# Products nobody reads, in the waits of TensorE, in a two-layer decoder trunk

## The reference, cut to what matters

```
x = x + gla_mixer(rmsnorm(x, c_norm[i]), c_w_in[i], c_w_a2[i], c_b_a[i], c_o_norm[i], c_w_out[i])
x = x + moe_ffn(rmsnorm(x, m_norm[i]), m_router[i], m_w_gate[i], m_w_up[i], m_w_down[i])
...
log_a = (jax.nn.log_sigmoid((a1 @ w_a2 + b_a).astype(jnp.float32)) / GLA_TAU).reshape(B, S, H, dk)
...
att = jnp.einsum('bhid,bhjd,bhijd->bhij', qc, kc, decay)
...
logits = (xt @ router).astype(jnp.float32)
top_v, top_i = lax.top_k(logits, TOP_K)
top_w = jax.nn.softmax(top_v, axis=-1)
```

## Time and profile before

| | |
|---|---|
| three executions | 1360.69, 1359.76, 1362.06 us |
| span of the profiled execution | 1358.3 us |
| TensorE products busy | 1297.8 us (96%) |
| weight loads busy | 1063.5 us (78%) |
| DVE, ACT, POOL busy | 1046.4, 814.9, 31.9 us |
| mean granted clock of TensorE | 0.973 |
| chain that ended last | PE 90%, DVE 5%, ACT 2%, issue 1%, POOL 1% |

### The profile page before, as it was taken

One profiled execution on the slowest core, in us unless ns is written; L12 is line 12 of the kernel. 1 busy time (PEld: TensorE's weight loads), 2 busy tenths in 40 slices (PEclk: granted clock), 3 DMA queues, 4 the chain that ended last, 5 costly groups with the idle time before them and its releaser, 6 DMA issues.

```text
span 1358.3 us, 17178 instructions
## 1 busy us (share of the span) xinstructions
PE 1297.8 (96%) x6105; PEld 1063.5 (78%) x6111; DVE 1046.4 (77%) x1014; ACT 814.9 (60%) x847; POOL 31.9 (2%) x29
## 2 busy tenths in 40 slices
PE   6999999999989997899999999999999999999997
PEld 5877878888778766688888888788887888888885
DVE  4786664444477945788998989889989889989986
ACT  5434354444335434577767767777776777777773
POOL 0130000000011000000000000000000000000000
PEclk9989999999989978799999999999999999999999
DMA  9540045554524302399999999999999899989992
GB/s 386 216 152 5 1 158 187 187 187 186 189 100 166 129 32 93 140 364 346 368 349 339 366 355 341 342 344 347 358 341 361 332 338 362 350 344 365 343 373 89
DMA packets 48635, 350.75 MB, mean 258 GB/s; under 512 B 5392, under 2 KB 5392, under 8 KB 6320
## 3 DMA queue, kind: packets, MB, share of 16 engines
q1 hardware_dynamic: 48560, 349.67, 68.5%
HBM read 348.60 MB, written 1.05 MB: 257 GB/s over the span
## 4 chain that ended last, share of the span: by engine, by line
PE 90%; DVE 5%; ACT 2%; issue 1%; POOL 1%; DMA 0%; SPq 0%; POOLq 0%; DVEq 0%; ACTq 0%
PE bank L490 26%; PE bank L492 26%; PE bank L491 26%; PE bank L922 1%; PE bank L652 1%; PE bank L798 1%; PE bank L678 1%; DVE wlo L1280 1%; ACT whi L1012 1%; PE bank L660 1%; PE bank L873 1%; PE bank L874 1%; PE bank L810 1%; PE bank L813 1%; PE bank L896 1%
## 5 line engine op out<-in xcount | busy, mean ns | idle before, releaser
L1854 DVE TENSOR_TENSOR wlo<-raw,whi 128x2048 fp32r<-128x2048 f32 x261 | 597.5, 2290 | 85.3 <-ACT whi L1207 82.2
L1207 ACT CAST whi<-raw 128x2048 fp32r<-128x2048 f32 x261 | 498.9, 1912 | 142.7 <-PE bank L492 142.3
L490 PE MATMUL bank<-whi,hT_hi 128*128 128x512 f32 (+1 forms) x1104 | 432.4, 392 | 9.2 <-DVE wlo L1280 3.9
L492 PE MATMUL bank<-whi,hT_lo 128*128 128x512 f32 (+1 forms) x1104 | 430.6, 390 | 2.7 <-issue 2.7
L491 PE MATMUL bank<-wlo,hT_hi 128*128 128x512 f32 (+1 forms) x1104 | 430.2, 390 | 0.0
L490 PEld LDWEIGHTS bank<-whi,hT_hi 128*128 128x128 f32 x1104 | 208.7, 189 | 55.1 <-issue 8.0
L1280 DVE TENSOR_TENSOR wlo<-raw,whi 128x2048 fp32r<-128x2048 f32 x68 | 155.7, 2291 | 122.3 <-ACT whi L1012 121.2
L492 PEld LDWEIGHTS bank<-whi,hT_lo 128*128 128x128 f32 x1104 | 208.5, 189 | 46.9 <-issue 3.6
L491 PEld LDWEIGHTS bank<-wlo,hT_hi 128*128 128x128 f32 x1104 | 208.6, 189 | 43.4 <-issue 0.2
L1012 ACT CAST whi<-raw 128x2048 fp32r<-128x2048 f32 x68 | 129.5, 1905 | 135.6 <-PE bank L492 135.4
L490 PE MATMUL bank<-whi,h_hi 128*128 128x512 f32 x440 | 181.6, 413 | 3.0 <-DVE h_lo L1543 3.0
(11 more groups left out here) (289 smaller groups left out, 979.1 us busy)
## 6 DMA issues: line engine op xcount, KB each, us to landing
raw<-in_weights SPq DMA_DIRECT2D x329, 1024.0 KB, 4.8
arena<-in_compress SPq DMA_DIRECT2D x1, 1088.0 KB, 14.6
x<-in_x SPq DMA_DIRECT2D x1, 1024.0 KB, 5.1
out<-x SPq DMA_DIRECT2D x2, 512.0 KB, 4.1
cst<-in_constants SPq DMA_DIRECT2D x1, 668.0 KB, 6.3
sml<-in_small SPq DMA_DIRECT2D x1, 402.0 KB, 6.8
msk_bits<-in_masks SPq DMA_DIRECT2D x1, 288.0 KB, 15.0
wa<-in_w_a SPq DMA_DIRECT2D x1, 64.0 KB, 15.0
```

What stands on the lines that cost most here:

```text
L490: mm(out_, a_hi, b_hi, start=start, stop=False)
L492: return mm(out_, a_lo, b_hi, start=False, stop=stop)
L1207: nc.scalar.copy(whi[:, u % SPLIT, :, :], raw[:, u % RAW, :, :]).then_inc(S["w_hi"], 1)
L1854: V.tensor_tensor(wlo[:, u % SPLIT, :, :], raw[:, u % RAW, :, :], whi[:, u % SPLIT, :, :].bitcast(F32), ALU.subtract).then_inc(S["w_lo"], 1)
```

## The change

A function `keep_busy(n, b)` issues n products of the mask with the identity into bank b. It is called at seven places with 9, 8, 9, 3, 12, 4 and 7 products, 52 in all. No bank so written is read before it is written anew, and no semaphore is waited for or counted up by the new products.

```diff
+            def keep_busy(n, b):
+
+                for _ in range(n):
+                    mm(bank[b][:, :], mident, msk[:, 0:512], start=True, stop=True)
...
             transposes(x, lambda i: pe.wait_ge(S["x_ready"], 4 + 2 * (i % 2) + i // 2 + 1))
+            keep_busy(9, 5)
             pe.wait_ge(S["sw_lo"], 2)
             small_products(3, sw_a1, bank[6][0:32, 0:SEQ]).then_inc(S["a1"], 1)
...
             cross(0)
+            keep_busy(8, 1)
             cross(1)
             diagonal(1)
...
             transposes(x, lambda i: pe.wait_ge(S["x_ready"], 8 + i + 1))
+            keep_busy(9, 5)
             small_products(5, sw_router, bank[4][0:16, 0:SEQ]).then_inc(S["logitsT_psum"], 1)
 
+            keep_busy(3, 5)
             pe.wait_ge(S["logitsT"], 1)
...
             last.then_inc(S["logits"], 1)
+            keep_busy(12, 5)
             pe.wait_ge(S["picked"], 1)
...
+            keep_busy(4, 5)
             pe.wait_ge(S["hn_lo"], 2)
             gather_rows(-1)
             gather(-1, 0)
             gather(-1, 1)
+            keep_busy(7, 5)
             expert(0, U_MOE, 0, fresh=True)
```

## The result

The changed kernel takes 1349.13 us, the median of six executions (1344.93 to 1350.30), beside 1360.22 of the kernel before (six executions, 1354.23 to 1363.53). The ratio is 0.9919, with a 95% interval from 0.9904 to 0.9934: 11.0 us less.

The account below looks back on a forecast made before the run. TensorE was taken to bound the kernel, full to the tail from about 580 us. Terms of 0, 2.0 (cross stretch) and 2.6 (routing) made 4.6 us off 1360.69, so 1356.1 us; range 1352.8 to 1360.2 us.

Parts of the forecast that it names:

- whatever moves the first product of `expert(0)` moves the end by as much: From about 580 us TensorE is full to the tail, so time won at the first expert reaches the end in full.
- my rivals: Four other outcomes: eight not raising the clock 0.22, both clocks up 0.18, gain and filling cancelling 0.10, slower 0.08.
- The nine before the low-rank product: In the 2.53 us wait there: nine fit and should keep the clock, but L761 waits for DVE; gain 0.
- The eight: Between cross(0) and cross(1): gain 2.0 us; 3.0 if they raise the clock, a loss of 0.9 if not.
- Counts and gather: Routing, fillings before counts and gather: counts 1.0 us earlier, `gather_rows` 1.85 us at full clock; 1.7 us gain, DVE the bound.
- The first expert: Seven products before the first expert: its first nine products at full clock would gain 1.9 us; half taken, 0.9.
- Filling in front of ready work: Rival: new products meet half clock in the routing and outlast waits; 2.6 us slower, 1363.3 us; chance 0.08.
- both clocks come up: Rival: eight raise the clock early, routing and first expert's start at full clock; 6.6 us gain, 1354.1 us; chance 0.18.

Follow-up runs that it names:

- e1: The narrow kernel: changed kernel with all 52 new products at their places, but 8 columns instead of 512; ratio 0.9972 to the kernel before.
- e9: Changed kernel with only the nine products before the low-rank product kept wide, the other 43 narrowed to 8 columns; ratio 0.9976 to the kernel before.
- e10: Changed kernel with only the eight products between cross(0) and cross(1) kept wide, all others narrowed to 8 columns; ratio 0.9948 to the kernel before.
- e2: Changed kernel with only the eight products between cross(0) and cross(1) left, the other calls deleted; ratio 1.0016 to the kernel before.
- e7: Changed kernel with 76 products of 8 columns more, 128 new products in all; 1352.01 us in a single execution.
- e8: Changed kernel with 33 wide products more, in waits it left open; ratio 0.9918 to the kernel before.
- e12: The changed kernel measured again, unaltered; 1349.31 us, ratio 0.9922 to the kernel before.
- e3: Changed kernel with only the 35 products of the routing and before the first expert left, the other calls deleted; ratio 0.9938 to the kernel before.
- e4: Changed kernel with only the nine products before the low-rank product left, the other calls deleted; ratio 1.0040 to the kernel before.
- e5: Kernel before with 16 products of 8 columns added in the wait before the low-rank product; ratio 1.0078 to the kernel before.
- e6: Kernel before with 18 products of 8 columns added in the wait before the low-rank product; ratio 1.0087 to the kernel before.

## Why the prediction was wrong, step by step

The step that failed is the sentence "whatever moves the first product of `expert(0)` moves the end by as much". The end moved by 3.6 us more. I had priced the new products as work and as clock, and not as code: they stand ahead of a loop, and moving the loop by 104 instructions took away two stops of 1.2 and 1.5 us, and with them 1.5 and 1.95 us of the distance. What ends such a stop is a block of code that lands. None of my rivals had this. The rows were there to see, 1.23 and 1.50 us of "issue" at the same product of the body, 200 us apart. Measured by the narrow kernel, this term, which the sum had at nothing, is 3.8 us of the 11.0.

The other terms were right in kind and two of them too small:

- *The nine before the low-rank product*: 0 forecast; 0.88 us of idle time ahead of the roots in the trace, and no difference between e9 and e1. Right.
- *The eight*: 2.0 forecast, a mean between 3.0 where they raise the clock and a loss of 0.9 where they don't. The trace has 2.98 at `diagonal(1)`, e10 3.3 us by its ratio, and the traces of e2 and e10 have 5.1 us at the first expert, of which 2.0 lie in the chain behind, to which I had given a microsecond either way. They raised the clock in every trace that had them wide (after, e2, e7, e8, e10 to e12), so the likelier case should have been taken and not the mean. That `cross(1)` falls back to half by itself was right, and it is why `diagonal(1)` won next to nothing (9.07 us for 9.2).
- *Counts and gather*: 1.7 forecast; 1.03 at `gather_rows` and 1.54 at DVE's L1824 (now L1836), counted from the counts. One sub-step was wrong: `gather_rows` ran at half clock, 3.49 us and not 1.85. It cost next to nothing: DVE's split ended at 545.37, and L1836 then waited 0.19 us for the first `gather`, so it was TensorE by a little, and not DVE as I had said. In e12, with `gather_rows` at full clock, `expert(0)` follows the counts by 10.63 us, for 10.86. The forecast had named DVE as the bound, and this saved it.
- *The first expert*: 0.9 forecast, half of 1.9. The trace has 1.81. I had let an idle time of 2 us between the gathers count against it. That was a misreading: 1.93 us is the distance from start to start (551.14 to 553.07) in the kernel before, and its idle time was 0.88 us there, as it is 0.87 now.
- *Filling in front of ready work*: nowhere. The twelve took 2.76 us and left 1.28 idle. Only the eight made something late, by 0.3 us.

Together the routing gave 4.6 us by the ratios (e3 beyond e1) and 3.5 by the trace, for 2.6. The clock's part is 6.56 us by the first trace, 8.3 by that of e12, and 7.2 by the ratios (0.9919 against 0.9972): the rival "both clocks come up" with its 6.6 us, to which I gave 0.18. `expert(0)` came 4.75 us earlier beyond the 1.93, where I had said 3.5 to 4. By the ratios 3.8 for the place, 3.3 for the eight and 4.6 for the routing are 11.7 us, for 11.0 measured; each of the three is uncertain by 1.6 to 3 us, so the sum is no close proof.

The rule of the Trainium skill ("TensorE: Matmul & The Clock Gate", Part 1) that the gate isn't started by the kernel and its changes lie elsewhere from one execution to the next is borne out: two executions differ by 1.93 us ahead of any edit. My use of it was wrong, since it moves the half-clock stretches of layer 0, and those behind the cross stretch (e12), rather than the chance that eight products raise the clock. Part 4 of the same page of the Trainium skill, by which the gate doesn't count a PE-mode transpose as work in the way it counts a product, had no occasion to show. I had taken from it that the seven products alone would have to raise the clock for the first expert, but it was up from 544.8 us, before the first of the eight transposes, and stayed up. Whether transposes help to keep it, no run here tells.

## What to carry to other kernels

When instructions are added or taken away ahead of a loop, look for "issue" time just behind the loop's jumps back, and find how far into the body it lies: the edit moves that point, and its cost here ran from 0 to some 16 us of 1360 without any change of work. To try an idea on such a kernel, keep its instruction count (narrow against wide products, at the same places), or a real gain of 3 us can measure as none (1.0016, e2), and a do-nothing edit as 5 us slower. Filling TensorE's waits pays where the products behind the wait set the end, here with products of 512 columns and not of 8; where another engine ends a later wait, the clock is kept for nothing.

## What the runs showed of the hardware that was not expected

- At a jump back in TensorE's program two instruction packets of 16 KB start 5.5 to 7.1 us apart (all 14 traces), and where the work up to the block's border runs out first, TensorE stops until 1.3 to 1.6 us after the second has landed: 5.3 to 5.5 us after the loop's first product at the first jump and 5.4 to 6.6 at the second (before, e2, e4, e5, e7), wherever its border lies. The pattern repeated after 256 instructions (e7).
- Most stops of 2.05 to 6.2 us there went with half clock: for 3.4 us in e2 (both jumps) and e8, and for 6.8 us in e5, e6 and at the second jump of e4. The first of e4, 3.37 us long, didn't, nor did those of 1.2 to 1.5 us.
- Products of 32 columns, back to back at full clock for 5.4 us, didn't keep the clock up here; nor did 10.3 us of them raise it. Eight of 512 columns between them were followed by full clock in each of the seven traces that had them, and in none of the seven others was it up there.
- The same kernel differed by 1.7 us between two executions by where its half-clock stretches fell (after and e12, 87.9 and 86.2 us from `cross(0)` to the expert's tenth product), beside the 1.93 us in layer 0.
